# Down projections by seven block products: 20 of 22 activation tiles, activation sums through DRAM

## What is computed

```python
h = rmsnorm(x, norm_ffn)
gu = h @ w_gate_up
x = x + (jax.nn.silu(gu[..., :D_FF]) * gu[..., D_FF:]) @ w_down      # D_FF = 2816 = 22 tiles of 128
hp = rmsnorm(x, norm_ple)
x = x + jax.nn.sigmoid(hp @ w_ple_gate) * (p_i @ w_ple_proj)
```

## Time and profile before

| | us |
|---|---|
| median of 3 runs (2496.17 to 2498.07) | 2496.22 |
| span of the profiled execution | 2494.5 |
| PE busy | 2467.6 |
| POOL busy | 992.5 |
| DVE busy | 1270.7 |
| ACT busy | 898.2 |

### The profile page before, as it was taken

How to read it: one execution, slowest core, us unless ns; L and a number is a source line. 1 busy time by engine, 2 the same in 40 slices (tenths; PEclk the granted TensorE clock), 3 DMA queues, 4 the chain that set the end, 5 groups by cost and what they waited for, 6 DMA issues and landing times.

```text
span 2494.5 us, 29698 instructions
## 1 busy us (share of the span) xinstructions
PE 2467.6 (99%) x11768; PEld 2037.2 (82%) x11768; DVE 1270.7 (51%) x1760; ACT 898.2 (36%) x1298; POOL 992.5 (40%) x596
## 2 busy tenths in 40 slices
PE   7999999999999999999999999999999999999998
PEld 6888888888888888888878887888888888888886
DVE  7967845543343352333596777545433433423335
ACT  4333334433333341125333252344433333322253
POOL 3211112278877832321221121223788877222120
PEclk9999999999999999999999999999999999999999
DMA  4342222123223252211143322311232223422111
GB/s 164 105 98 65 71 85 85 45 84 92 76 77 91 87 195 107 78 50 44 38 154 98 78 56 67 102 59 60 80 93 81 76 85 110 150 110 70 51 49 70
DMA packets 89370, 214.43 MB, mean 86 GB/s; under 512 B 34568, under 2 KB 43016, under 8 KB 84880
## 3 DMA queue, kind: packets, MB, share of 16 engines
q1 hardware_dynamic: 61456, 126.90, 16.9%
q10 hardware_dynamic: 27776, 85.63, 10.0%
HBM read 163.70 MB, written 35.68 MB: 80 GB/s over the span
## 4 chain that ended last, share of the span: by engine, by line
PE 97%; DVE 1%; ACT 1%; issue 0%; DMA 0%; POOL 0%; ACTq 0%; DVEq 0%; POOLq 0%
PE proj L1986 20%; PE proj L1987 20%; PE proj L1988 20%; PE proj L2090 5%; PE aux L2090 5%; PE aux L2089 5%; PE proj L2089 5%; PE aux L2088 5%; PE proj L2088 5%; PE aux L2205 1%; PE aux L2224 1%; PE aux L2215 1%; PE aux L2310 0%; PE aux L2315 0%; PE aux L2281 0%; PE aux L2268 0%
## 5 line engine op out<-in xcount | busy, mean ns | idle before, releaser
L1937 POOL TENSOR_TENSOR w_lo<-w_raw,w_hi 128x1024 fp32r<-128x1024 f32 (+1 forms) x144 | 367.2, 2551 | 1256.5 <-ACT w_hi L1468 1256.4
L1986 PE MATMUL proj<-h_hi,w_hi 128*128 128x512 f32 x1760 | 694.8, 395 | 0.9 <-POOL w_lo L1937 0.9
L1988 PE MATMUL proj<-h_lo,w_hi 128*128 128x512 f32 x1760 | 685.5, 389 | 0.0
L1987 PE MATMUL proj<-h_hi,w_lo 128*128 128x512 f32 x1760 | 685.1, 389 | 0.0
L1986 PEld LDWEIGHTS proj<-h_hi,w_hi 128*128 128x128 f32 x1760 | 330.4, 188 | 72.4 <-issue 3.1
L1988 PEld LDWEIGHTS proj<-h_lo,w_hi 128*128 128x128 f32 x1760 | 330.3, 188 | 69.2
L1987 PEld LDWEIGHTS proj<-h_hi,w_lo 128*128 128x128 f32 x1760 | 330.5, 188 | 68.8 <-issue 2.4
L1468 ACT ACTIVATE w_hi<-w_raw 128x1024 fp32r<-128x1024 f32 (+1 forms) x143 | 146.5, 1026 | 440.5 <-PE proj L1988 295.9
L1025 DVE TENSOR_TENSOR x<-x,proj 128x512 f32<-128x512 f32 x128 | 87.7, 687 | 405.6 <-PE proj L1988 405.3
L1944 POOL TENSOR_TENSOR w_lo<-w_raw,w_hi 128x512 fp32r<-128x512 f32 x120 | 183.5, 1531 | 88.5 <-ACT w_hi L1450 88.5
L1944 POOL TENSOR_TENSOR w_lo<-turns,w_hi 128x512 fp32r<-128x512 f32 x120 | 180.4, 1504 | 62.9 <-ACT w_hi L1450 62.9
(11 more groups left out here) (290 smaller groups left out, 4161.3 us busy)
## 6 DMA issues: line engine op xcount, KB each, us to landing
w_raw<-weights SPq DMA_DIRECT2D x168, 512.0 KB, 3.7
act_spill<-act ACTq DMA_DIRECT2D x44, 512.0 KB, 5.5
turns<-weights SPq DMA_DIRECT2D x40, 512.0 KB, 4.4
h_whole<-act_spill ACTq DMA_DIRECT2D x12, 1024.0 KB, 8.1
ffn_b_whole<-act_spill ACTq DMA_DIRECT2D x8, 1024.0 KB, 5.5
w_raw<-weights SPq DMA_DIRECT2D x16, 384.0 KB, 3.1
ml_d<-rows_spill ACTq DMA_DIRECT2D x64, 64.0 KB, 3.4
rows<-ret_qkv ACTq DMA_DIRECT2D x32, 128.0 KB, 2.3
```

Of the source, the lines that this page charges most:

```text
L1937: g.tensor_tensor(wlo[:, slot, 0:n], w, whi[:, slot, 0:n].bitcast(F32), ALU.subtract).then_inc(weights_ready.sem, 1)
L1986: pe.matmul(out, wh, rhi, start=first, stop=False)
L1987: pe.matmul(out, wl, rhi, start=False, stop=False)
L1988: return pe.matmul(out, wh, rlo, start=False, stop=final)
```

## The change

Two of the 22 activation tiles keep the plain form: two `wide` units, 16 fills of 2 tiles x 3 matmuls. The other 20 go in five parts of four tiles. For each part and each half of the output channels (two groups of 7, `NDB = 10` groups in all) seven block products are made, each of 2 x 2 x 3 = 12 matmuls into two PSUM banks (`down_group`). `down_banks(g)` gives x two banks of `proj` in turn, z the first two and y the last two of `aux`. DVE adds or subtracts the banks after every product straight into x (`down_add`, 128x1024). The products need sums of activations: DVE makes one 128x512 sum after each even block and three after each odd one (`act_sums`, in `rows`), ACT's queue stores them with the tiles (`store_block`), and `load_part` brings back seven pieces of 512 KB per part, which ACT and DVE split as before. POOL makes the four weight sums and seven lows per group as in a block. The squares for the next norm (`ple_square`) and the highs and lows of the next product move between the adds of the last two groups, in another order; the two halves of p (`p_whole`, `p_first`) get places of their own; the clearing of `rows` in layer 0 and the reload of `turns` move later.

The diff, cut:

```diff
-PARTS = [range(0, 8), range(8, 14), range(14, 22)]
+DPARTS = 5
+NDB = 2 * DPARTS
 U_GATES, U_MQ, U_MK, U_MV, U_MO, U_RG, U_POOL, U_RET, U_OUT, U_FFN = 0, 1, 4, 7, 10, 13, 16, 18, 27, 35
 U_DN = U_FFN + 2 * NSTD
-U_PROJ = U_DN + 8 * len(PARTS)
+U_PROJ = U_DN + 2
...
+KEPT = {M_A11: 0, M_S4: 1, M_A12: 2, M_S1: 3, M_S2: 4, M_S3: 5, M_A22: 6}
...
+def blocks_before(u):
+    if u == U_DN:
+        return range(NBS)
+    return range(NBS, NBS + NDB) if u == U_PROJ else ()
...
+    sums_d = nc.dram_tensor("act_sums_spill", (P, 2 * DPARTS, 7, HALF), F32, kind="Internal").ap()
...
+            def act_sums(L, b):
+                p = b // 2
+                t = [t_four(j) for j in range(4)]
+                f = NSTD + b
+                for h in range(2):
+                    v.wait_ge(act_made.sem, act_made.at(L, 2 * f + 2))
+                if b % 2 == 0:
+                    v.wait_ge(sums_stored.sem, sums_stored.at(L, 16 * p))
+                    v.tensor_tensor(t[0], act_t[:, 0, 1, :], act_t[:, 0, 0, :], ALU.subtract).then_inc(act_summed.sem, 1)
+                    return
+                v.tensor_tensor(t[1], act_t[:, 1, 0, :], t[0], ALU.add).then_inc(act_summed.sem, 1)
+                v.tensor_tensor(t[2], t[1], act_t[:, 0, 1, :], ALU.subtract).then_inc(act_summed.sem, 1)
+                v.tensor_tensor(t[3], act_t[:, 1, 1, :], t[1], ALU.subtract).then_inc(act_summed.sem, 1)
...
                     up_first(L, b)
+                    gate_second(L, b)
                     if b == NBS - 1:
                         act_low(L, 0)
                         act_low(L, 1)
-                    gate_second(L, b)
-                    if b == NBS - 1:
-                        for f in range(2, 6):
-                            act_low(L, f)
                     up_second(L, b)
-                    if b == NBS - 1:
-                        act_low(L, 6)
-                        act_low(L, 7)
                     gate_first(L, b)
                     v.wait_ge(up_scaled.sem, up_scaled.at(L, 2 * b + 2))
                     finish_act(L, NSTD + b, 1)
                     finish_act(L, NSTD + b, 0)
+                    act_sums(L, b)
...
+            def down_add(L, g, i):
+                x_bank, z_bank, y_bank = down_banks(g)
+                bank_of = (x_bank, z_bank, x_bank, y_bank, x_bank, y_bank, x_bank)[i]
+                h = (1, 1, 0, 0, 0, 0, 1)[i]
+                to = x[:, down_tiles(g, i in (0, 1, 2, 5)), hs(h)]
+                v.wait_ge(product_done.sem, product_done.at(L, operand_at(NBS + g, i)))
+                if i in (1, 4, 5):
+                    v.wait_ge(down_added.sem, down_at(L, g, {1: 0, 4: 3, 5: 2}[i]))
+                v.tensor_tensor(to, to, bank_of, ALU.subtract if i in (3, 5) else ALU.add).then_inc(down_added.sem, 1)
...
             def ffn_down(L):
-                if L == 0:
-                    v.memset(rows[:, :, :], 0.0).then_inc(rows_clear, 1)
...
-                v.wait_ge(act_stored.sem, act_stored.at(L, 16 * FT))
                 for k in range(16):
-                    n, h = divmod(k, 2)
-                    add_fill(L, U_DN + 16 + n, h, OUT_LAST[n], h)
...
-                add_square(L, 16, 15)
-                for c, h in PLE_PIECES[8:]:
-                    ple_low(L, c, h)
+                    add_fill(L, U_DN + k // 8, k % 8, k // 2, k % 2)
+                    if k % 2 and k < 14:
+                        act_low(L, NSTD + k // 2)
+                for k in (6, 7):
+                    v.wait_ge(emptied[bank(U_DN + 1, k)].sem, emptied_at(L, U_DN + 1, k))
+                for g in range(NDB):
+                    for i in range(7):
+                        down_add(L, g, i)
+                        if g < NDB - 2 and (i >= 4) == (g % 2 == 0):
+                            act_low(L, NSTD + 7 * (g // 2 + 1) + (i - 4 if g % 2 == 0 else i + 3))
+                        elif g == NDB - 2:
+                            if i in (2, 3):
+                                p_low(L, i - 2)
+                            if i == 5:
+                                for j in range(4):
+                                    ple_square(L, j)
+                            if i == 6:
+                                ple_square(L, 4)
+                        elif g == NDB - 1:
+                            if i == 0:
+                                ple_square(L, 5)
+                                ple_square(L, 6)
+                            if i == 1:
+                                ple_square(L, 7)
+                            if i == 2:
+                                ple_lows(L, 0, 2)
...
+                for j in range(12, 16):
+                    ple_square(L, j)
+                ple_lows(L, 7, 16)
...
+            def store_block(L, b):
+                p = b // 2
+                a.wait_ge(act_made.sem, act_made.at(L, 2 * (NSTD + b) + 2))
+                if b % 2 == 0:
+                    a.dma_start(sums_d[:, p, 0, :], act_t[:, 0, 1, :]).then_inc(even_stored.sem, 16)
+                    return
+                a.dma_start(sums_d[:, p, 1:3, :], act_t[:, 1, :, :]).then_inc(odd_stored.sem, 16)
+                a.wait_ge(act_summed.sem, act_summed.at(L, 4 * p + 4))
+                a.dma_start(sums_d[:, p, 3:7, :], rows.rearrange("p a (k c) -> p (a k) c", k=2)).then_inc(sums_stored.sem, 16)
...
+            def load_part(L, q, i):
+                pairs = 2 * DPARTS - 1 if q == 0 else 2 * DPARTS
+                a.wait_ge(stored.sem, stored.at(L, 16 * pairs))
+                if q == 1 and i in (M_A11, M_A12):
+                    a.wait_ge(unit_done.sem, unit_done.at(L, U_DN + 2))
+                elif q > 1:
+                    a.wait_ge(product_done.sem, product_done.at(L, operand_at(NBS + 2 * (q - 2) + 1, i)))
+                to = part_place(i, q % 2)[2].rearrange("p (j c) -> p j c", j=2)
+                a.dma_start(to, sums_d[:, 2 * q:2 * q + 2, KEPT[i], :]).then_inc(act_landed[i].sem, 16)
...
-                        highs_ahead(L, k + 6)
+                        if k + 6 < 7 * NBS:
+                            highs_ahead(L, k + 6)
                         if last:
-                            for u in range(U_DN, U_DN + RING):
-                                if max(key[3] for key in TOOK[("unit", L, u)][1] if key[2] == b) == i:
-                                    units_high(L, u)
+                            if i in (2, 4):
+                                units_high(L, U_DN + (i - 2) // 2)
+                            if i in (5, 6):
+                                highs_ahead(L, 7 * NBS + i - 5)
+                            if i < 2:
+                                load_plain(L, i)
+                            load_part(L, 0, i)
                         if i == 1:
-                            store_act(L, NSTD + b - 1)
-                        if last and i < 4:
-                            load_pair(L, 0, i)
-                        if last:
-                            for f in {2: (0, 1), 4: (2, 3, 4, 5), 5: (6, 7)}.get(i, ()):
-                                act_high(L, f)
+                            if b == 0:
+                                store_plain(L, 1)
+                            else:
+                                store_block(L, b - 1)
+                        if last and i == 4:
+                            act_high(L, 0)
+                            act_high(L, 1)
...
+                store_block(L, NBS - 1)
                 for i in range(3):
-                    load_pair(L, 1, i)
+                    act_high(L, NSTD + i)
+                a.wait_ge(unit_done.sem, unit_done.at(L, U_DN + 1))
+                highs_ahead(L, 7 * NBS + 2)
+                highs_ahead(L, 7 * NBS + 3)
+                for i in range(3, 7):
+                    act_high(L, NSTD + i)
+                a.wait_ge(unit_done.sem, unit_done.at(L, U_DN + 2))
+                highs_ahead(L, 7 * NBS + 4)
+                highs_ahead(L, 7 * NBS + 5)
+                for g in range(NDB):
+                    q, second = divmod(g, 2)
+                    for i in range(7):
+                        k = 7 * (NBS + g) + i
+                        a.wait_ge(product_done.sem, product_done.at(L, k + 1))
+                        highs_ahead(L, k + 6)
+                        if q < DPARTS - 1:
+                            if not second:
+                                load_part(L, q + 1, i)
+                            if (i >= 4) == (not second):
...
+                            for u in range(U_PROJ, U_PROJ + RING):
+                                if max(key[3] for key in TOOK[("unit", L, u)][1] if key[2] == NBS + g) == i:
+                                    units_high(L, u)
+                            if i == 0:
+                                for j in range(5, 8):
+                                    ple_square(L, j)
...
+                for j in range(14, 16):
+                    ple_square(L, j)
                 if L < DEPTH - 1:
```

(87 more changed lines are left out.)

295 lines of the change are left out of this document (147 added, 148 removed).

## The result

The kernel after takes 2521.88 us (median of four runs, 2511.84 to 2526.91) beside 2497.06 us before: 1.0095 times, 95% interval 1.0084 to 1.0107. It is slower, where 2469 us, a faster kernel, was forecast. The execution that was profiled is the fastest of the four; its span is 2510.1 us, 15.6 us over the one of before.

The account below looks back on a forecast made before the run. PE, busy 99% of the span, was taken as the bound: 2494.5 - 54.4 + 12 + 11 + 4 = 2467 us of span, so a median of 2469 us, with a range of 2446 to 2499 us.

Parts of the forecast that it names:

- Fewer matmuls: Down projections: 936 instead of 1056 matmuls per layer, 240 fewer in all at 0.2265 us each, -54.4 us.
- POOL, DMA, blocks at 0: POOL's sums and lows, the loads and the blocks' extra store sums all stay hidden behind PE, cost 0.
- The rival with POOL as the bound: Down groups: POOL's work exceeds the 38.1 us that two groups last, losing 40 us in all; 2482 us, chance 0.13.
- DVE's new add at 1.2 us: Down groups: DVE's 128x1024 add from PSUM into x takes 1.2 us, bounds 1.15 and 1.37.
- The subtraction beside POOL: Down groups: DVE's activation-low subtraction, 1.22 us, meets POOL about 8 times in 10 and waits some 0.5 us.
- The rival in which every subtraction waits for a whole POOL operation: Down groups: DVE and POOL fall into step, 3.7 us per product instead of 2.72; 2507 us, slower, chance 0.12.
- Bursts: Down groups: seven subtractions between adds make DVE late, 1.5 us each time, eight times; +12 us, bounds 0 and 43.
- the paragraph on ACT and DMA: Down groups: ACT's highs and DMA issues take about 10 of 19 us, loads land in time; cost 0, one hazard noted.
- Entry: From blocks to plain part: fifth fill waits for a late DVE add, 6 to 7 and 4 us; +11, bounds 4 and 18.
- Exit: Last down group: DVE's backlog, then ACT's copies of the projections, 2 us per layer; +4 us, bounds 0 and 10.
- All hidden: Whole change: other engines' work stays behind PE, 5 to 8 us lost in all; 2449 us, chance 0.25.

Follow-up runs that it names:

- the best version: Kernel after with three edits: late activation high before the weight high, last block's activation sums behind plain fills, PLE lows behind the last add; 2456.45 us, ratio 0.9839.
- without the lock: Kernel after with the groups' activation-low subtraction replaced by a one-input reduction of the same size, leaving the subtraction out; 2484.99 us, ratio 0.9950.
- The edit to the lows: Kernel after with DVE making the seven PLE lows after the last down group instead of between its adds; 2511.04 us, ratio 1.0057.
- the long artificial waits: Kernel before with eight PE waits in its down stage, each for DVE's add and four idle additions; 2555.74 us, ratio 1.0235.

## Why the prediction was wrong

- **Fewer matmuls, -54.4 us**: right. 11528 matmuls against 11768, at 0.226 us in the groups of the best version, whose PE is busy 2416.1 us where this term gives 2413.2.
- **POOL, DMA, blocks at 0**: right. POOL is busy 308.1 us between 503 and 884 us as before, and no new wait of PE names it or a landing. The rival with POOL as the bound is out.
- **DVE's new add at 1.2 us**: right, 1.205 to 1.222 us over 140 of them. The subtraction beside POOL: the median is 1.47 us for `h_lo` against 1.2 alone, the mean over all 74 is 1.51, so a mean wait of 0.3 us where 0.5 was taken. The rival in which every subtraction waits for a whole POOL operation did not come about; that the kernel came out slower, as this rival had it, has another cause.
- **Bursts, +12 us**: this is the step that failed. It gave 1.5 us per burst and the trace shows 3.5 in each of the eight, 28 of the 34.1 us. The sum counted DVE's work, 19.2 us without and 22.7 with waits against 21.8, as if only DVE's rate decided. The hazard that did decide is named in the paragraph on ACT and DMA ("ACT's high for k+6 is queued ahead of the activation high and can wait for POOL's sums"), was seen in rows with 47.7 us over 20 times, and was priced at 0 there and at most at 0.5 us in a burst; in the blocks nothing hangs on it. In the groups it does: DVE's low hangs on that high, and the add that PE needs stands behind the low. In the sum of the burst the lock was looked at from DVE's side only; it also delays POOL's sums, by 2.1 us in a burst, and that is what ACT then passes on: without the lock 0.7 of the 3.5 us stay, and with ACT's order changed none of a burst's gap does.
- **Slow matmuls**: a term that was missing, 19.4 us in the profiled execution, some 15 of them the lower clock and 3 the counting of the pauses. The median of the runs is 10 us longer and lies between two at a lower mean clock (0.985 and 0.987 beside 0.991), so I estimate some 30 there. Without it the kernel after would lie at 2490.7 us of span, within the range and no slower than before. The sum had gaps of 6 to 7 us in it and treated PE after them as if nothing had happened. None of the rows ahead of the prediction shows a slow stretch; the first 20 us of the trace of before do. The reading of the earlier trace rows hid that part: 0.9 us is the idle time in front of L1986 alone, while PE idles 26.9 us in all, 11.8 of them at L1993 near the start. For the stretches that the change touches the reading holds.
- **Entry, +11 us**: right in size (12.1 of waiting and 1.3 of issue) and in mechanism: the fifth plain fill waited 6.8 us in layer 0 and 5.3 in layer 1 for adds behind DVE's three sums, and moving `act_sums` away takes the longest wait to 1.8 us. What was missing is again the clock behind it.
- **Exit, +4 us**: half of what it came to. The edit to the lows took 6.0 us of waits for adds away, and 2.1 stood at `ple_in`: 8 us over both layers.

Beside the matmuls' gain the span took 15.6 + 54.4 = 70 us where 27 were forecast. Of the 43 us between, the bursts are 28 - 12 = 16, the ends 4, the entry 2.4, the waits at `aux` 1.0 and the busy time beyond the count 19.4. "All hidden", 2449 us, with a chance of 0.25, is 7 us from what the reordered kernel does; but it was a forecast for the kernel as written, and failed there.

## What to carry to other kernels

When work is added in front of an in-order engine, follow the queue and not the sum: for each instruction that the bounding engine waits for, list what stands ahead of it on its engine, and what each of these waits for, through every engine. A wait that is harmless where it is seen (here 47.7 us on ACT) has to be priced anew where something urgent now stands behind it. On PE, a few long gaps can cost more than their length, so breaking gaps of 3.5 us down to 0.7 us gained more than 2.8 us each.

## What was not expected of the hardware

Behind a long pause of TensorE its granted clock is at the lower level for a few microseconds, and the length matters more than the sum: eight waits of 3.8 to 5.8 us were each followed by such a stretch and added 2.4 us of busy time each, eight of 1.5 us were followed by none. Waits of 3.5 us lie between the two. Of eight such waits, four were followed by a slow stretch in the profiled execution of the kernel after, all eight where the sums of the last block were moved, and six where the PLE lows were. This fits the spread of the runs: the same kernel after ran from 2511.84 to 2526.91 us at mean granted clocks of 0.991 down to 0.984, while the runs with the long artificial waits stay within 2 us, and those of the version without long gaps within 2.3. Length is not all of it: near the start of the kernel before, where PE had worked for some 5 us so far, a pause of 2.1 us was followed by 3 us at a clock of 0.51. Which of several equal gaps is followed by a slow stretch was not found out.
